# Delta rule on one core: the next pair's strict product among the last levels of the current inverse, pairs planned 43 instead of 48.12 units apart

## The reference, cut to what matters

```
def rwkv7_scan(r, w, k, v, kk, a):
    def step(state, inp):
        r_t, w_t, k_t, v_t, kk_t, a_t = inp
        sa = jnp.einsum('bhvk,bhk->bhv', state, -kk_t)
        state = (state * w_t[:, :, None, :]
                 + sa[..., None] * (kk_t * a_t)[:, :, None, :]
                 + v_t[..., None] * k_t[:, :, None, :])
        return state, jnp.einsum('bhvk,bhk->bhv', state, r_t)
    ...
    y = rwkv7_scan(r_h, w_h, k_h, v_h, kk, a_h)
    mean = jnp.mean(y, axis=-1, keepdims=True)
    var = jnp.mean(jnp.square(y - mean), axis=-1, keepdims=True)
    y = ((y - mean) * lax.rsqrt(var + LNX_EPS)).reshape(b, s, RWKV_W) * lnx_g + lnx_b
    bonus = jnp.sum(r_h * k_h * r_k, axis=-1, keepdims=True) * v_h
    y = (y + bonus.reshape(b, s, RWKV_W)) * g
```

## Time and profile before

| | us |
|---|---|
| median of 3 runs | 3192.43 |
| lowest, highest | 3192.25, 3195.77 |
| the profiled execution, its own time | 3188.94 |
| its span | 3187.1 |
| stage from pair 2's inverse to the output projection (1630.68 to 1811.75) | 181.07 |
| one pair in it (1669.13 to 1707.59) | 38.46 |

### The profile page before, as it was taken

One profiled execution on the slowest core, in us unless ns is written; L12 is line 12 of the kernel. 1 busy time (PEld: TensorE's weight loads), 2 busy tenths in 40 slices (PEclk: granted clock), 3 DMA queues, 4 the chain that ended last, 5 costly groups with the idle time before them and its releaser, 6 DMA issues.

```text
span 3187.1 us, 43936 instructions
## 1 busy us (share of the span) xinstructions
PE 3130.6 (98%) x18180; PEld 2483.1 (78%) x18180; DVE 1709.3 (54%) x2577; ACT 1207.6 (38%) x1919; POOL 475.0 (15%) x393
## 2 busy tenths in 40 slices
PE   9999999999999999999999999999999999999999
PEld 6776778877777888887777788888888887678887
DVE  6965557845556443347877544335474334554333
ACT  4355534535543422233344432223352224442221
POOL 0022112013110310113322021011011001021110
PEclk9999999999999999999999999999999999999999
DMA  6765224346332233342100143333323322033332
GB/s 248 245 186 139 74 99 131 114 117 171 91 105 67 93 98 94 99 122 93 61 2 2 42 132 97 100 95 97 88 91 100 98 88 83 8 96 93 99 99 80
DMA packets 103498, 321.62 MB, mean 101 GB/s; under 512 B 10488, under 2 KB 26116, under 8 KB 101124
## 3 DMA queue, kind: packets, MB, share of 16 engines
q1 hardware_dynamic: 80564, 275.82, 27.7%
q10 hardware_dynamic: 22736, 43.00, 5.1%
HBM read 311.41 MB, written 9.72 MB: 101 GB/s over the span
## 4 chain that ended last, share of the span: by engine, by line
PE 86%; DVE 4%; ACT 3%; issue 1%; POOL 0%; DMA 0%; ACTq 0%; DVEq 0%; POOLq 0%
PE acc L498 72%; PE acc L1596 1%; PE acc L2619 1%; PE acc L2605 1%; PE aux L1907 1%; PE aux L1918 1%; PE aux L3404 1%; PE acc L1931 1%; PE acc L2106 1%; PE aux L2095 1%; DVE w_lo L409 1%; DVE ssd_ex L1493 0%; PE acc L390 0%; ACT w_hi L402 0%; PE acc L3438 0%
## 5 line engine op out<-in xcount | busy, mean ns | idle before, releaser
L498 PE MATMUL acc<-op_hi,w_hi 128*128 128x512 f32 x2624 | 1068.5, 407 | 5.0 <-DVE op_lo L1226 2.0
L402 ACT ACTIVATE w_hi<-raw 128x1024 fp32r<-128x1024 f32 (+2 forms) x476 | 494.3, 1039 | 1468.8 <-PE acc L498 1451.8
L498 PE MATMUL acc<-op_lo,w_hi 128*128 128x512 f32 x2624 | 1024.9, 391 | 0.0
L498 PE MATMUL acc<-op_hi,w_lo 128*128 128x512 f32 x2624 | 1024.5, 390 | 0.0
L409 DVE TENSOR_TENSOR w_lo<-raw,w_hi 128x1024 fp32r<-128x1024 f32 (+2 forms) x476 | 578.9, 1216 | 251.8 <-ACT w_hi L402 251.2
L498 PEld LDWEIGHTS acc<-op_hi,w_hi 128*128 128x128 f32 x2624 | 493.6, 188 | 146.1 <-issue 46.9
L498 PEld LDWEIGHTS acc<-op_lo,w_hi 128*128 128x128 f32 x2624 | 494.3, 188 | 105.3 <-issue 9.8
L498 PEld LDWEIGHTS acc<-op_hi,w_lo 128*128 128x128 f32 x2624 | 493.5, 188 | 105.8
L498 PE MATMUL acc<-ffn_hi,w_hi 128*128 128x512 f32 x800 | 311.4, 389 | 0.0
L498 PE MATMUL acc<-ffn_hi,w_lo 128*128 128x512 f32 x800 | 311.2, 389 | 0.0
L498 PE MATMUL acc<-ffn_lo,w_hi 128*128 128x512 f32 x800 | 311.2, 389 | 0.0
(11 more groups left out here) (595 smaller groups left out, 3551.9 us busy)
## 6 DMA issues: line engine op xcount, KB each, us to landing
raw<-in_w SPq DMA_DIRECT2D x436, 512.0 KB, 3.6
late_ada<-in_ada ACTq DMA_DIRECT2D x32, 512.0 KB, 4.3
raw<-in_w SPq DMA_DIRECT2D x32, 384.0 KB, 3.0
ssd_ex<-cum ACTq DMA_DIRECT2D x16, 512.0 KB, 5.4
ssd_ex<-cum ACTq DMA_DIRECT2D x16, 384.0 KB, 6.6
ada<-in_ada ACTq DMA_DIRECT2D x4, 1024.0 KB, 14.2
ada<-in_ada SPq DMA_DIRECT2D x4, 1024.0 KB, 22.7
ssd_ex<-cum ACTq DMA_DIRECT2D x16, 256.0 KB, 5.1
```

What stands on the lines that cost most here:

```text
L402: act.activation(self.w_hi[g % AHEAD][:, 0:k, :], self.raw[s][:, 0:k, :], ACT.Copy).then_inc(self.split_hi.handle, 1)
L498: mm = pe.matmul(self.bank(s, g), w[:, k, :], a[:, k, 0:s.n], start=(k == 0 and q == 0), stop=(k == k_tiles - 1 and q == 2))
```

## The change

Three things change in the numbers. `PAIR` goes from 48.12 to 43, which brings everything of pair m + 1 nearer to pair m; the front is now written relative to the inverse before it, and stays where it was beside that (-37.16 + 48.12 = 10.96). The strict product, and with it its copies on DVE and ACT and POOL's start matrices, gets a due time of its own for pairs 2 to 5: 22.6 after the front, 9.4 units ahead of the other three products. The chunks are planned 5.5 instead of 5.73 units apart, and the norm at 28.9 instead of 29.56. The two numbers of the memory attention change as well.

```diff
-    LEVELS, PAIR = 6, 48.12
-    AT = {"front": -37.16, "products": 32.0, "product": 1.61, "turns": 4.06, "turn": 3.1, "bonus": 23.11,
+    LEVELS, PAIR = 6, 43.0
+    AT = {"front": 10.96, "strict": 22.6, "products": 32.0, "product": 1.61, "turns": 4.06, "turn": 3.1, "bonus": 23.11,
...
-          "chunk": 5.73, "chunk_out": 2.32, "correct": 0.58, "move": 3.6, "norm": 29.56, "y": -1.95, "center": 1.6,
+          "chunk": 5.5, "chunk_out": 2.32, "correct": 0.58, "move": 3.6, "norm": 28.9, "y": -1.95, "center": 1.6,
...
-                self.tA.append(self.t1[0] + 4 * at["turn"] + 2.0 if m == 1 else self.tB[m - 1] + self.PAIR + at["front"])
+                self.tA.append(self.t1[0] + 4 * at["turn"] + 2.0 if m == 1 else self.tB[m - 1] + at["front"])
...
     def product_time(self, m, i):
+        if i == 0 and m > 1:
+            return self.tA[m] + self.AT["strict"]
         return self.tP[m] + (self.AT["product"] if m else 3.4) * i
...
         def bases(m):
-            yield self.tP[m] + self.AT["base"]
+            yield self.product_time(m, 0) + self.AT["base"]
...
-    memory.times(rwkv.tB[-1] + 15.0, rwkv.tB[-1] + 45.0, [rwkv.out_done.ge(RW - 2), rwkv.turn_kept.ge(4 * RW)],
+    memory.times(rwkv.tB[-1] + 20.3, rwkv.tB[-1] + 44.34, [rwkv.out_done.ge(RW - 2), rwkv.turn_kept.ge(4 * RW)],
```

## The result

| | before | after |
|---|---|---|
| median of the runs, us | 3193.18 (4 runs, 3192.25 to 3195.77) | 3235.41 (4 runs, 3234.16 to 3243.39) |
| ratio | | 1.0136, interval 1.012 to 1.0152 |
| span of the profiled execution | 3187.1 | 3234.9 |
| first matmul of the output projection | 1811.75 | 1859.56 |

The kernel became slower by 42 us; 3216 was predicted, with a range of 3200 to 3227. The sign was right, the size was not. The profiled executions differ by 47.8 us in span, and just as much in the start of the output projection. Of this 2.1 us are there already at the last L498 ahead of the stage (1576.05 and 1578.11), where the lists are still the same, and have nothing to do with the change; the other 45.8 us arise in the stage that the prediction speaks of.

The account below looks back on a forecast made before the run. PE, busy 98% of the span, was taken as the bound, so only its idle time or added work counts. Terms 16.6 + 4.2 + 0.4 + 2.4 gave +23.6 on 3188.94, 3212.5, or 3216 on the median's scale; range 3200 to 3227.

Parts of the forecast that it names:

- The chain through DVE at the solves: Strict product to L2667: DVE's work ahead of the gate makes PE idle 5.3 us against 2.5, +2.8 at four places.
- Mean and level group: Behind the last chunk: the mean waits for ACT's copy of y, +0.78, the second level group +0.56, at four places.
- Level 2 behind the copies of product 3: First group of level 2 waits because DVE's level 1 update stands behind product 3's copies: +0.8 at three places.
- the correction: State correction L2698: a group of turns now stands behind it instead of ahead, so PE's wait grows +0.6 at three places.
- The sum without the clock: Added idle time of PE in the stage and memory attention, without clock loss; a period of the stage goes from 38.46 to 44.0.
- the stretch with the memory attention: Pair 5: one norm group moves behind level 6; between -1.2 and +2, taken as +0.4.
- The clock: PE's clock may fall in the new idle stretches: 0.6 at each of four places, +2.4, bounds 0 and 6.8.
- the upper bound of 1.7 per place: Most the low clock could cost at each of four places, 6.8 in all, judged from rows of the last attention.
- Rival C: Clock stays low for much of the four gaps, level groups and chunks behind: some 10 us above the sum, 3226; chance 0.12.
- The rule of the Trainium skill: Half clock comes only after a whole idle stretch, so idle pieces of 2 us at most cost nothing; sum 2.4 smaller.
- part 2: Chunks and norm closer: +0.78 at the mean and +0.56 at the level group, four places; +0.6 before the correction, three places.

Follow-up runs that it names:

- The mended DVE order: Changed kernel with only DVE's list altered in pairs 2 to 5: level 5 of head 0 before the strict product's copies, next inverse's start after the norm; 3223.57 us, 1.0105.
- the kernel with the waits filled: Changed kernel plus matmuls whose result nobody reads, placed where PE waits around the solves and before the first state correction; 3221.02 us, 1.0089 to the kernel before.
- filled alone: Changed kernel plus 6 unused matmuls only before the first state correction of pairs 0 to 3; 3225.16 us, 1.0103 to the kernel before.
- filled at the solves: Changed kernel plus unused matmuls only around the solves (level 6, L2661, L2669), none before the correction; 3232.89 us, 1.0125 to the kernel before.
- norm and turns: Changed kernel with chunk 5.73, norm 29.56 and the turns of pairs 2 to 5 5.12 units earlier, as before beside the chunks; 3224.13 us, 1.0098.
- the two together: Changed kernel with DVE's list reordered around the solves, and norm, chunks and turns put back as in the kernel before; 3200.22 us, 1.0028.
- late turns: Kernel before with only the turns of pairs 2 to 4 5.12 units later, one group behind the first state correction; 3199.70 us, 1.0021.
- close norm: Kernel before with only the norm's mean and gate of pairs 0 to 3 right behind the last chunk on PE; 3194.84 us, 1.001.

## Why the prediction was right and wrong, step by step

- **The chain through DVE at the solves: right.** 13.6 worked out, 13.65 measured at full clock, with the waits and releasers named. The mended DVE order, which moves nothing on PE, took it away.
- **Mean and level group: right.** 0.78 and 0.56 worked out, 0.70 and 0.48 measured; alone in the kernel before they give +2.5 us (0.1%, interval 0.01 to 0.20) and 4.5 in the stage of the profiled execution.
- **Level 2 behind the copies of product 3: wrong.** 0.8 worked out, 0.05 measured. It is offset by the correction, 0.6 worked out, 0.9 measured, with 0.22 before a level group beside it that I had left out.
- **The sum without the clock: right for a period, somewhat small for the stage.** A period is 43.6 to 43.8 against 44.0. For the whole, 21.2 was worked out, and the kernel with the waits filled has some 26.5. A part is in the stretch with the memory attention, taken as +0.4: from the last solves to the output projection it grew by 2.1 (33.04 to 35.17, at full clock).
- **The clock: the step that failed**, "I take 0.6 for each of four places, +2.4, as DVE is the one that sets the pace there and a slow PE loses nothing while it waits for DVE". Five low stretches of 61.4 us together made PE's work 29.5 us longer. A part of that took the place of idle time, which grew by 16.2 only where 21.2 were worked out. What is loss by the clock is 24.6 us, if the sum's idle time is taken from the 45.8, and some 19 by the kernel with the waits filled: eight to ten times the 2.4. The step failed in three ways. The clock did not come back when the waits ended: 16.4 of the 17.1 us were busy (window 1701.30 to 1718.40). The reason given holds in part at the solves, where 13.7 us of low clock cost 4.4 (the difference of two kernels' pairs, above); behind the correction, where PE hardly waits, 17.1 us of it cost 7.1, and there the sum had no term for the clock at all. And the upper bound of 1.7 per place was taken from one low stretch of 3.4 us in the last attention; nothing said that this was an upper bound, and the same code has one of 17.1 us in four other executions. Rival C named the mechanism, with some 12 us for the clock in all.
- **The wait before the correction** I had priced at its own length. In the changed kernel it heads the longest low stretches; filled alone it gave back 10 us.
- **The rule of the Trainium skill** ("TensorE: Matmul & The Clock Gate", section "The HAM clock gate"), as I had read it, leaves the clock alone with idle pieces of 2 us at the most. The trace does not agree: the pieces ahead of each fall are 0.2 to 1.8 us long (rows of the timeline above). The same page, section "A second HAM failure mode: psum-queue depth-cycling", tells of a kernel in which short pauses between groups of matmuls made the clock swing; the trace agrees with that, with five falls in this stage. I had not weighed it.
- **The range.** Its stated parts, added to 3216, give 3209 to 3225 and not 3203 to 3223: -1.6, -2.4 and -2.9 below, +1.6, +4.4 and +2.9 above (2.9 is 30% of the 9.6 of part 2 and the level 2 wait). The measured 3235 lies outside of either.

## What to carry to other kernels

When a change adds waits to a part in which the engine runs mostly small matmuls, price the clock with the work that follows, not only with the wait: in this case one wait of 1.53 us was followed by no low stretch or by up to 17.1 us of one, so the term deserves a range of that width. A low stretch seen once is no upper bound. Filling the waits with matmuls of no use is a cheap way to split idle time from clock. And when a product is moved earlier, read the list of the engine that copies it out: its copies go ahead of whatever was the next thing to be waited for. Here only the order in which level 5, the copy of the inverse and the norm come first, together with products as cover on PE, gave the gain.

## What the runs showed of the hardware that was not expected

- The clock stayed at 1.2 GHz for 17 us with PE busy for 16.4 of 17.1 us. Small matmuls only ran in it up to mean and gate; other low stretches ended among small ones (13.7, 10.2 and 3.4 us, PE busy throughout).
- Low stretches behind the same wait of 1.53 us were 3.4, 6.8, 10.2, 13.7 and 17.1 us long, and there was none in the first pair of the changed kernel. With the very list of the changed kernel behind the wait they were 3.4 (filled at the solves), 10.2 (DVE's order mended), 13.7 and 17.1. So neither the wait nor the list behind it tells whether and for how long the clock falls; what does, isn't settled, and the turns behind the wait are not shown to be what kept the stretches short in the kernel before.
- The last attention, the same in all kernels, had low stretches of 0 to 17.1 us. A part of the spread between executions of one kernel may come from this; no run here separates it.
- In the changed kernel norm and turns gave 11 us, DVE's order 12, the two together 35: more than the sum, as each left the low stretches of the other kind or longer ones. In the kernel before, late turns and close norm add up within the noise (0.21% and 0.10% against 0.45%, interval 0.30 to 0.59).
